# A state space mixer: the transposes of a group's inputs go behind its first projection, and VectorE scales the preceding group's output before it scales these inputs

## The chip, the cores and the metric

The kernel runs on one core of a Trainium2 chip. The time is the device time in microseconds of one execution; what is compared are medians of several executions. The engines named below are TensorE (PE in the rows; its weight loads are PEld), VectorE (DVE), ScalarE (ACT), GpSimd (POOL) and SyncE (SP, which only issues DMAs). All arithmetic is float32.

## The reference

One inference step of a two-layer decoder trunk, for a prompt of 512 tokens and for 8 samples with caches. Layer 0 is dilated attention beside gated linear attention, then an MLP. Layer 1 is the Mamba-2 state space mixer, then an MLP. The change lies in the mixer of layer 1:

```
z, xbc, dt = split_cols(h @ w_in, (C_INNER, C_CONV_DIM, C_HEADS))
conv = depthwise causal convolution of xbc over 4 taps
xbc_c = jax.nn.silu(conv + conv_b)
xs, bm, cm = split_cols(xbc_c, (C_INNER, C_GROUPS * C_STATE, C_GROUPS * C_STATE))
...
xdt = x * dt[..., None]
cb = einsum('bntgk,bnsgk->bngts', cm, bm)
y_intra = einsum('bngts,bngjts,bnsgjp->bntgjp', cb, seg, xdt)
u = einsum('bnsgk,bnsgj,bnsgjp->nbgjpk', bm, to_end, xdt)
...
y = y + d_skip[:, None] * xs
y = y.reshape(bsz, t_len, C_INNER) * jax.nn.silu(z)
y = rms_norm(y per group, w_gnorm)
```

There are 8 groups of 4 heads; a group has 256 channels of `x`, 128 of `B`, 128 of `C`, 256 of `z`. The 512 prompt tokens form four chunks of 128.

## The kernel before

Features lie on partitions and tokens along the free axis (520 columns: 512 of the prompt, 8 samples). A projection unit (`unit`, L535) multiplies 1024 features by 128 output columns in 16 matmuls, 8 for columns 0 to 259 and 8 for 260 to 519; its 512 KB of weights come by DMA into a ring of slots (`ring`). Each group needs six units: two for `x`, one for `B`, one for `C`, two for `z`.

The mixer is a software pipeline over groups. While group g is mixed, the six units of group g+1 are projected. Every engine has its own program, written out in order, with semaphores between them; groups 1 to 6 are a loop of three rounds with two groups each, groups 0 and 7 stand outside.

TensorE runs `ssd_mix`: transposes of `B` and of the samples (`ssd_tokens`, L966, L968) and of the inputs `x` (L974) from features to tokens, unit 0, the product of `C` and `B` (`ssd_cb`, L982), units 1 and 2, unit 3 with the samples' little products between its matmuls (`sample_y`, L995), the products inside and between chunks (L1011, L1016, L1025) among units 4 and 5, and last the sums of squares for the norm of the group's output (`ssd_norm`, L1032). In the last group `out_ahead` (L1089), the first part of the output projection, takes the place of the units.

The transposed `x` goes to PSUM banks 4 and 5. The same banks have just held the sums of squares of the preceding group, which ScalarE reads for its roots `ystd` (L1405, L1407); so the transposes wait for the semaphores `y_std_low` and `y_std`, which ScalarE gives.

VectorE runs `mix`: it copies the group's table (`tabg`, L1971) and the samples' rows (`ssamp`, L1975), scales these by dt (`sxdt`, L1976), scales the transposed `x` by dt (`xdt`, L1981, two instructions that read banks 4 and 5), then `normed` for the preceding group: a reciprocal (`yrstd`, L1948) and two products (`yout`, L1950, which read `yT` and `yrstd` from SBUF). Then the skip product (L1996), `prepare` and `taps` for the next group (L1898 to L1910: the convolution of one block of 128 channels, which needs that ScalarE has copied that unit's bank to `xe`), `xde` (L2000), `cbm` (L2003), `finish` (L1916, which needs ScalarE's tanh), the second block's taps, and `step_states` (L1992), eight instructions that step the samples' states `ss0`. TensorE's unit 3 waits for these (semaphore `ssm_stepped`, in `sample_y`).

GpSimd runs `states`: once `sxdt` is written it sends it to DRAM and back with a broadcast (L484, L488), and then multiplies the samples' states by their decays in two instructions on `ss0` (L496); it also sends states out and in.

The loops' order is only that of the code; nothing reorders it. The lines of the change:

```
dve.wait_ge(sem("x_turned"), g + 1)          # before xdt
dve.wait_ge(sem("y_std"), g + 1)             # at the start of normed
pe.wait_ge(sem("y_std" if t else "y_std_low"), g)   # before the transposes of x
pe.wait_ge(sem("ssm_stepped"), g * 2 + 2)    # in sample_y, before unit 3
```

Of the kernel before, what the change touches and what calls it, by code (L numbers as in the profile page):

```python
# [16 lines left out]
ALU = mybir.AluOpType  # L17
# [3 lines left out]
P = 128  # L21
# [23 lines left out]
CG, CHD, CN = 8, 64, 128  # L45
CJ = 4
# [97 lines left out]
def build(nc, A):  # L144
    ctx = ExitStack()
    with ctx:
        sems = {}

        def sem(name):
            if name not in sems:  # L150
                sems[name] = ctx.enter_context(nc.semaphore(name))
            return sems[name]

        def sb(name, shape, dt=F32, stack=ctx):
            return stack.enter_context(nc.sbuf_tensor(name, shape, dt))
# [123 lines left out]
        xdt = sb("xdt", [P, NT, CJ, CHD], stack=c)  # L279
# [243 lines left out]
        def _(pe):  # L523
            mm = nc.tensor.matmul

            def unit(w, n, s, count, src, first=0, last=True, start=True, ready=None, blocks=range(DC), used=True,
                     between=None):


                pe.wait_ge(ring_in[s], count * 16)  # L530
                for cols, half in MATMULS:
                    for k in blocks:
                        if ready is not None:
                            pe.wait_ge(*ready(k, cols.start > 0))
                        x = mm(half(n), ring[:, s, k], src[:, first + k, cols],  # L535
                               start=start and k == blocks[0], stop=last and k == blocks[-1])
                        if between is not None and not (cols.start and k == blocks[-1]):
                            between(k + DC * (cols.start > 0))
                x.then_inc(units_multiplied if used else sem("parts_multiplied"), 1)

            def bank_free(n, more=0):

                if n >= 2:
                    pe.wait_ge(copied[n % 2], turns_before(n) + more)
# [8 lines left out]
            def normed(r):  # L553

                return lambda k, high: (hn_ready, HN_BEFORE[r] + k + 1 + (0 if r in LATE_ROOT else DC * high))
# [7 lines left out]
            def project():  # L563

                w = at[0]
                if w >= U_OUT0:
                    return
                at[0] += 1
                n = T_ATT + w if w < U_GLA else T_GLA + w - U_GLA
                if w == U_GLA:  # L570
                    gates()
                bank_free(n)
                unit(w, n, w % RING, w // RING + 1, hn,
                     ready=normed(0) if w == 0 else None)

            def gates():

                n = T_GATE
                bank_free(n)
                pe.wait_ge(late_consts_in, 16 * len(LATE_CONSTS))  # L580
                for cols, half in MATMULS:
                    for k in range(DC):
                        x = mm(half(n)[0:RANK], wglow[:, k], hn[:, k, cols], start=k == 0, stop=k == DC - 1)
                x.then_inc(sem("glow_summed"), 1)
# [377 lines left out]
            def ssd_tokens(g, d):  # L962

                pe.wait_ge(sem("conv_ready"), g + 1)
                for t in range(NT):
                    pe.transpose(B[6][:, t * P:(t + 1) * P], conv[:, d, 2, t * P:(t + 1) * P], ident[:])  # L966
                for i in range(2):
                    x = pe.transpose(B[7][0:NB, i * P:(i + 1) * P], conv[:, d, i, TP:T], ident[:])  # L968
                x.then_inc(sem("ssd_turned"), 1)
                for t in range(NT):  # L970
                    if t % 2 == 0 and (not isinstance(g, int) or g > 0):
                        pe.wait_ge(sem("y_std" if t else "y_std_low"), g)
                    for i in range(2):
                        x = pe.transpose(B[4 + t // 2][:, (t % 2) * GW + i * P:(t % 2) * GW + (i + 1) * P],  # L974
                                         conv[:, d, i, t * P:(t + 1) * P], ident[:])
                x.then_inc(sem("x_turned"), 1)

            def ssd_cb(g, d):

                pe.wait_ge(sem("btok_ready"), g + 1)  # L980
                for t in range(NT):
                    x = mm(B[6][:, t * P:(t + 1) * P], conv[:, d, 2, t * P:(t + 1) * P],  # L982
                           conv[:, d, 3, t * P:(t + 1) * P], start=True, stop=True)
                x.then_inc(sem("cb_ready"), 1)

            def sample_y(g, d, products):


                pe.wait_ge(sem("cbm_ready"), g + 1)
                pe.wait_ge(sem("ssm_stepped"), g * 2 + 2)  # L990

                def some(m):
                    for n in range(m * 2 * NB // (products - 1), (m + 1) * 2 * NB // (products - 1)):
                        i, b = n // NB, n % NB
                        x = mm(B[6][:, n:n + 1], flat(ss0[:, b, 2 * i:2 * i + 2, :]),  # L995
                               conv[:, d, 3, TP + b:TP + b + 1], start=True, stop=True, skip_group_check=True)
                        if n == 2 * NB - 1:
                            x.then_inc(sem("ssm_read"), 1)
                return some
# [20 lines left out]
            def ssd_inter(g, d):  # L1020

                pe.wait_ge(sem("states_kept"), g + 1)
                for t in range(1, NT):
                    for i in range(2):
                        x = mm(B[4 + i][:, t * P:(t + 1) * P], flat(st[:, t - 1, 2 * i:2 * i + 2]),  # L1025
                               conv[:, d, 3, t * P:(t + 1) * P], start=True, stop=True)
                x.then_inc(sem("y_inter"), 1)
# [7 lines left out]
            def ssd_mix(g, d, project, products=2 * DC):  # L1035

                if not isinstance(g, int) or g > 0:
                    pe.wait_ge(sem("y_read"), g)
                ssd_tokens(g, d)
                project(0)  # L1040
                ssd_cb(g, d)
                project(1)
                project(2)
                project(3, sample_y(g, d, products))
                ssd_intra(g)
                project(4)
                ssd_inter(g, d)
                project(5)
                ssd_norm(g)
# [389 lines left out]
        def _(dve):  # L1439
            V = nc.vector  # L1440
# [451 lines left out]
            def mdo(ins, name=None):  # L1892
                mix_tally.done(ins, mstep if name is None else sem(name))

            def prepare(g, d):

                conv_tally.start("conv", g)
                cdo(V.tensor_scalar(pg[:, d, 0:20], parm[:, g, 0:20], 0.5, None, ALU.mult))  # L1898
                cdo(V.tensor_copy(pg[:, d, 20:24], parm[:, g, 20:24]))
                cdo(V.tensor_copy(xs[:, :, 0:3, :], parm[:, g, 24:120].rearrange("p (c t b) -> p c t b", c=4, t=3)))  # L1900

            def taps(g, d, j):

                n = T_SSD + j
                dve.wait_ge(copied[n % 2], g * (SSD_UNITS // 2) + (turns_before(n) + 1))
                out = conv[:, d, j, 0:TP]
                cdo(V.tensor_scalar(out, xe[:, j, 0:TP], pg[:, d, 4 * j:4 * j + 1], pg[:, d, 16 + j:17 + j],
                                    ALU.mult, ALU.add))
                for tap in range(1, TAPS):
                    cdo(V.scalar_tensor_tensor(out, xe[:, j, tap:tap + TP], pg[:, d, 4 * j + tap:4 * j + tap + 1],  # L1910
                                               out, ALU.mult, ALU.add), "taps_done" if tap == TAPS - 1 else None)
# [46 lines left out]
            def pair(i):  # L1958
                return B[i][:].rearrange("p (t j q) -> p t j q", t=2, j=CJ)
# [5 lines left out]
            def mix(g, d, nxt, prev):  # L1965
                mix_tally.start("mix", g)
                dve.wait_ge(sem("ssd_turned"), g + 1)
                if prev is not None:
# [3 lines left out]
                steps = tabg[:, F_DT:F_CUM].rearrange("p (t j) -> p t j", j=CJ)  # L1972
# [3 lines left out]
                mdo(V.tensor_tensor(sxdt[:], ssamp[:].rearrange("b i (j q) -> b (i j) q", j=2),  # L1976
                                    steps[0:NB, NT].unsqueeze(2).to_broadcast((NB, CJ, CHD)), ALU.mult),
                    "sxdt_ready")
                dve.wait_ge(sem("x_turned"), g + 1)
                for i in range(2):  # L1980
                    mdo(V.tensor_tensor(xdt[:, 2 * i:2 * i + 2], pair(4 + i),  # L1981
                                        steps[:, 2 * i:2 * i + 2].unsqueeze(3).to_broadcast((P, 2, CJ, CHD)),
                                        ALU.mult), "xdt_ready" if i else None)
                if prev is not None:
                    normed(prev, 1 - d)
                def step_states(half):
# [9 lines left out]
                    mdo(V.tensor_scalar(yT[:, i], conv[:, d, i], pg[:, d, 20 + i:21 + i], None, ALU.mult))  # L1996
                if nxt is not None:
                    prepare(nxt, 1 - d)
                    taps(nxt, 1 - d, 0)
                mdo(V.tensor_tensor(xde, xdt[:], toend[:].unsqueeze(3).to_broadcast((P, NT, CJ, CHD)),  # L2000
                                    ALU.mult), "xde_ready")
# [257 lines left out]
```

## Time and profile before

| | |
|---|---|
| median of 3 executions | 1883.25 us (1878.39, 1883.25, 1883.38) |
| the profiled execution | 1877.73 us, of which the span is 1875.9 us |
| busy over the span | TensorE 95%, its weight loads 81%, VectorE 54%, ScalarE 21%, GpSimd 7% |
| mean granted TensorE clock | 0.963 of full speed |
| the mixer's eight groups | about 923 to 1384 us of the span |

TensorE is busy nearly throughout, so the time is its work plus the stops in it. An engine with a lower share matters only where TensorE waits for it. In the timeline rows the first number is the start and the second the duration, from the first instruction of the merged row to the end of its last; in brackets stands how long the engine was idle before it and who released it. A matmul in float32 leaves two records, so a unit of 16 matmuls shows as x32.

### The profile page before, as it was taken

What the parts mean: (1) busy time and instruction counts of PE and PEld (TensorE: products, weight loads), DVE (VectorE), ACT (ScalarE), POOL (GpSimd) and SP (SyncE); (2) the same over time, 40 slices, a digit from 0 to 9 for tenths busy, and PEclk for the clock granted to TensorE, in tenths of its full rate; (3) what the DMA queues carried; (4) which work ended last, traced back from release to release, by engine and by line L of the source; (5) the groups of instructions that cost most, each with busy time, mean ns of one, the idle gap of its engine ahead of it and who ended that gap; (6) DMA issues with size and microseconds to landing.
All of it is one profiled execution on the core that took longest, in us unless ns stands there. A gap on an engine that the chain in (4) does not pass through costs nothing.

```text
span 1875.9 us, 23013 instructions
## 1 busy us (share of the span) xinstructions
PE 1783.4 (95%) x8520; PEld 1512.1 (81%) x8520; DVE 1018.9 (54%) x1889; ACT 389.1 (21%) x964; POOL 128.9 (7%) x205
## 2 busy tenths in 40 slices
PE   6999999997999999998999999999999999999995
PEld 5776688776888888887888888888878888888884
DVE  4443762437554445445477777777652543454554
ACT  2332101101220023100143432334310230012100
POOL 1000210000000000000101111101100000000001
PEclk9999968878999999998999999999999999999997
DMA  7111532103654675551333343432322332443211
GB/s 253 63 56 46 177 109 63 36 13 112 238 199 153 239 284 216 195 203 34 132 131 113 118 146 137 148 126 101 140 100 79 141 137 115 157 157 135 96 62 46
DMA packets 50168, 244.25 MB, mean 130 GB/s; under 512 B 7544, under 2 KB 10696, under 8 KB 44960
## 3 DMA queue, kind: packets, MB, share of 16 engines
q1 hardware_dynamic: 37312, 123.74, 19.4%
q0 software_dynamic: 12624, 119.21, 16.5%
q8 instruction: 60, 0.98, 0.2%
q14 instruction: 28, 0.23, 0.1%
q10 hardware_dynamic: 144, 0.09, 0.0%
HBM read 227.56 MB, written 82.53 MB: 165 GB/s over the span
## 4 chain that ended last, share of the span: by engine, by line
PE 84%; DVE 9%; DMA 2%; issue 2%; ACT 2%; POOL 0%; DVEq 0%; ACTq 0%; SPq 0%
PE bank L922 41%; PE bank L535 28%; PE bank L1089 2%; PE bank L677 1%; DVE ss L1992 1%; DVE conv L1910 1%; PE bank L1011 1%; PE bank L637 1%; PE bank L621 1%; PE bank L995 1%; DVE rstd L1450 1%; PE bank L1016 1%; DMA ring<-units 1%; DVE yrstd L1948 1%; DMA gath<-cache_v 1%
## 5 line engine op out<-in xcount | busy, mean ns | idle before, releaser
L535 PE MATMUL bank<-hn,ring 128*128 128x260 f32 x2304 | 552.8, 394 | 13.4 <-DVE ss L1992 6.5
L535 PEld LDWEIGHTS bank<-hn,ring 128*128 128x128 f32 x2304 | 434.6, 194 | 87.8 <-issue 16.1
L922 PE MATMUL bank<-hid,ring 128*128 128x260 f32 x1024 | 231.0, 383 | 0.0
L922 PEld LDWEIGHTS bank<-hid,ring 128*128 128x128 f32 x1024 | 194.7, 190 | 29.7
L922 PE MATMUL bank<-hid,ssum 128*128 128x260 f32 x768 | 174.2, 382 | 0.0
L922 PEld LDWEIGHTS bank<-hid,ssum 128*128 128x128 f32 x768 | 146.0, 190 | 22.3
L922 PE MATMUL bank<-hn,ring 128*128 128x260 f32 x512 | 125.1, 387 | 5.6 <-DVE hnt L1727 5.6
L922 PE MATMUL bank<-hnt,ring 128*128 128x260 f32 x512 | 123.5, 383 | 0.0
L1747 DVE TENSOR_TENSOR u<-bank,p1c 128x260 f32<-128x260 f32 x48 | 20.6, 429 | 185.1 <-PE bank L922 183.5
L922 PE MATMUL bank<-hnt,ssum 128*128 128x260 f32 x512 | 118.9, 385 | 1.8 <-DVE hid L1756 1.8
L922 PEld LDWEIGHTS bank<-hn,ring 128*128 128x128 f32 x512 | 98.4, 193 | 21.6 <-DVE hnt L1727 6.4
L922 PEld LDWEIGHTS bank<-hnt,ssum 128*128 128x128 f32 x512 | 97.8, 191 | 17.3 <-DVE hid L1756 2.2
L922 PEld LDWEIGHTS bank<-hnt,ring 128*128 128x128 f32 x512 | 97.6, 191 | 15.0
L1290 ACT ACTIVATE hid<-hid 128x260 f32<-128x260 f32 x96 | 40.3, 420 | 258.2 <-DVE hid L1753 178.4
L1752 DVE TENSOR_TENSOR u<-bank,u 128x260 f32<-128x260 f32 x48 | 20.6, 428 | 122.9 <-PE bank L922 122.6
L1137 ACT ACTIVATE hn<-h 128x520 f32<-128x520 f32 x40 | 25.0, 635 | 261.2 <-DVE h L1783 153.4
L1910 DVE SCALAR_TENSOR_TENSOR conv<-xe,pg,conv 128x512 f32<-128x512 f32 x96 | 72.2, 752 | 3.4
L535 PE MATMUL bank<-mixT,ring 128*128 128x260 f32 x224 | 60.7, 433 | 9.4 <-DVE h L1699 9.3
L1302 ACT ACTIVATE p1c<-bank 128x260 f32<-128x260 f32 x48 | 18.6, 387 | 244.9 <-PE bank L922 244.9
L535 PEld LDWEIGHTS bank<-mixT,ring 128*128 128x128 f32 x224 | 47.5, 216 | 23.6 <-DVE h L1699 11.8
L922 PE MATMUL bank<-hn,ssum 128*128 128x260 f32 x256 | 61.3, 382 | 0.0
L535 PE MATMUL bank<-yout,ring 128*128 128x260 f32 x256 | 56.4, 383 | 2.4 <-DVE h L1699 2.4
(341 smaller groups left out, 2188.7 us busy)
## 6 DMA issues: line engine op xcount, KB each, us to landing
ring<-units SPq DMA_DIRECT2D x224, 512.0 KB, 4.1
seg<-cums POOLq DMA_DIRECT2D x8, 1024.0 KB, 4.8
ss<-ssm POOLq DMA_DIRECT2D x8, 1024.0 KB, 7.5
xb<-sxs POOLq DMA_DIRECT2D x8, 1024.0 KB, 5.0
out_ssm<-ss POOLq DMA_DIRECT2D x8, 1024.0 KB, 5.8
out_win_k<-cache_k POOLq DMA_DIRECT2D x8, 1022.0 KB, 8.5
out_win_v<-cache_v POOLq DMA_DIRECT2D x8, 1022.0 KB, 6.3
gath<-cache_k POOLq DMA_DIRECT2D x24, 256.0 KB, 3.9
```

What stands on the lines that cost most here:

```text
L535: x = mm(half(n), ring[:, s, k], src[:, first + k, cols], start=start and k == blocks[0], stop=last and k == blocks[-1])
L621: mm(B[4 + j][:, 0:(j + 1) * P], qr[rows, j * P:(j + 1) * P], kr[rows, 0:(j + 1) * P], start=True, stop=True).then_inc(sem("scored"), 1)
L637: mm(B[7][AD * e:AD * e + AD, kt * P:TP], vtok[:, kt, AD * e:AD * e + AD], pt[:, PT_AT[kt]:PT_AT[kt] + TP - kt * P], start=kt == 0, stop=k ...
L677: x = mm(out[:, hp, b, :], gath[:, n % SLOTS, i, hp * P:(hp + 1) * P], spt[:, i, b * AH + 2 * hp:b * AH + 2 * hp + 2], start=b == 0 and hp ...
L922: x = mm(bank[:, 0:LO], weight(m, w, q % (DC // 2)), operand(m, q), start=q == 0 and m not in (2, 3), stop=q == every - 1, skip_group_chec ...
L995: x = mm(B[6][:, n:n + 1], flat(ss0[:, b, 2 * i:2 * i + 2, :]), conv[:, d, 3, TP + b:TP + b + 1], start=True, stop=True, skip_group_check= ...
L1089: x = mm(bank(n), ring[:, w, k], yout[:, part * DC + k, cols], start=part == 0 and k == 0, stop=part == 1 and k == DC - 3, skip_group_chec ...
L1137: run(hn[:, k], h[:, k], ACT.Square).then_inc(squares, 1)
L1290: ins = run(out, src, ACT.Relu)
L1747: do(V.tensor_tensor(u2[:], B[5][:, 0:LO], p1c[:], ALU.add), "banks_read")
L1752: do(V.tensor_tensor(u3[:], B[7][:, 0:LO], u2[:], ALU.add), "banks_read")
L1910: cdo(V.scalar_tensor_tensor(out, xe[:, j, tap:tap + TP], pg[:, d, 4 * j + tap:4 * j + tap + 1], out, ALU.mult, ALU.add), "taps_done" if t ...
```

## The change

On TensorE the eight transposes of `x` leave `ssd_tokens` and become `ssd_inputs`, called behind `project(0)`. Their waits for `y_std_low` and `y_std` go with them. On VectorE the wait for `x_turned` and the two `xdt` products go behind `normed`, the skip product and `prepare`, ahead of the first `taps`. The other engines' programs are the same. No instruction is added or removed.

```
--- before.py
+++ after.py
@@ ssd_tokens
                 x.then_inc(sem("ssd_turned"), 1)
+
+            def ssd_inputs(g, d):
+
                 for t in range(NT):
                     if t % 2 == 0 and (not isinstance(g, int) or g > 0):
                         pe.wait_ge(sem("y_std" if t else "y_std_low"), g)
@@ ssd_mix
                 ssd_tokens(g, d)
                 project(0)
+                ssd_inputs(g, d)
                 ssd_cb(g, d)
@@ mix on VectorE
-                dve.wait_ge(sem("x_turned"), g + 1)
-                for i in range(2):
-                    mdo(V.tensor_tensor(xdt[:, 2 * i:2 * i + 2], pair(4 + i),
-                                        steps[:, 2 * i:2 * i + 2].unsqueeze(3).to_broadcast((P, 2, CJ, CHD)),
-                                        ALU.mult), "xdt_ready" if i else None)
                 if prev is not None:
                     normed(prev, 1 - d)
@@ mix on VectorE, behind the skip product
                 if nxt is not None:
                     prepare(nxt, 1 - d)
+                dve.wait_ge(sem("x_turned"), g + 1)
+                for i in range(2):
+                    mdo(V.tensor_tensor(xdt[:, 2 * i:2 * i + 2], pair(4 + i),
+                                        steps[:, 2 * i:2 * i + 2].unsqueeze(3).to_broadcast((P, 2, CJ, CHD)),
+                                        ALU.mult), "xdt_ready" if i else None)
+                if nxt is not None:
                     taps(nxt, 1 - d, 0)
```

TensorE at the start of a group of the loop, before: L966 and L968 are the transposes of `B` and of the samples, L974 those of `x`, L535 unit 0, L982 the product of `C` and `B`.

```order
L966 MATMUL bank<-ident,conv 128x128 x3
L968 MATMUL bank<-ident,conv 8x128 x2
L974 MATMUL bank<-ident,conv 128x128 [waits y_std_low]
...
L974 MATMUL bank<-ident,conv 128x128 [waits y_std]
...
L535 MATMUL bank<-hn,ring 128x260 [waits ring0_in]
L535 MATMUL bank<-hn,ring 128x260 x15
L982 MATMUL bank<-conv 128x128 [waits btok_ready]
```

The same place after the change, where L977 is the old L974 and L985 the old L982.

```order
L966 MATMUL bank<-ident,conv 128x128 x3
L968 MATMUL bank<-ident,conv 8x128 x2
...
L535 MATMUL bank<-hn,ring 128x260 [waits ring0_in]
L535 MATMUL bank<-hn,ring 128x260 x15
L977 MATMUL bank<-ident,conv 128x128 [waits y_std_low]
...
L977 MATMUL bank<-ident,conv 128x128 [waits y_std]
...
L985 MATMUL bank<-conv 128x128 [waits btok_ready]
```

The transposes of `x` and both their waits have moved past the 16 matmuls of unit 0.

VectorE at the start of a group of the loop, before: from the samples' product to the first tap of the next group.

```order
L1976 TENSOR_TENSOR sxdt<-ssamp,tabg 8x256 [waits ssamp_read]
L1981 TENSOR_TENSOR xdt<-bank,tabg 128x512 [waits x_turned,sxdt_ready]
...
L1981 TENSOR_TENSOR xdt<-bank,tabg 128x512 [waits vec_ssd_step]
L1948 RECIPROCAL yrstd<-ystd 128x520 [waits y_std,xdt_ready]
...
L1950 SCALAR_TENSOR_TENSOR yout<-yT,pg,yrstd 128x520
...
L1996 TENSOR_SCALAR yT<-conv,pg 128x520 [waits yout_ready]
...
L1900 COPY xs<-parm 128x4x24
...
L1907 TENSOR_SCALAR conv<-xe,pg 128x512 [waits pair0_copied]
```

The same place after the change (L1980 is the old L1976, L1952 and L1954 are L1948 and L1950, L1995 is L1996, L1904 is L1900, L2000 is L1981, L1911 is L1907).

```order
L1980 TENSOR_TENSOR sxdt<-ssamp,tabg 8x256 [waits ssamp_read]
L1952 RECIPROCAL yrstd<-ystd 128x520 [waits y_std,sxdt_ready]
...
L1954 SCALAR_TENSOR_TENSOR yout<-yT,pg,yrstd 128x520
...
L1995 TENSOR_SCALAR yT<-conv,pg 128x520 [waits yout_ready]
...
L1904 COPY xs<-parm 128x4x24
...
L2000 TENSOR_TENSOR xdt<-bank,tabg 128x512 [waits x_turned,vec_conv_step]
...
L2000 TENSOR_TENSOR xdt<-bank,tabg 128x512 [waits vec_ssd_step]
...
L1911 TENSOR_SCALAR conv<-xe,pg 128x512 [waits pair0_copied]
```

The reciprocal follows the samples' product directly, and the two `xdt` products stand between `prepare` and the first tap.

## Rows read from the trace of the kernel before

**Rows 1.** The page's first line.
```profile
span 1875.9 us, 23013 instructions
```

**Rows 2.** Timeline: the sums of squares that close groups 0 and 6.
```profile
980.48 1.04 PE L1032 MATMUL bank<-turns,normc 128*128 128x260 f32 x4
1324.81 1.04 PE L1032 MATMUL bank<-turns,normc 128*128 128x260 f32 x4
```

**Rows 3.** All waits of TensorE's matmuls from 980 to 1330 us: total, times, longest.
```profile
PE bank L974 <- ACT ystd L1405: 7.7, 7, 1.1
PE bank L535 <- DVE ss L1992: 6.5, 6, 1.2
```

**Rows 4.** Timeline of TensorE in group 3.
```profile
1098.05 1.09 PE L974 MATMUL bank<-ident,conv 128*128 128x128 f32 x8 [1.11 <-ACT ystd L1405]
1098.98 7.18 PE L535 MATMUL bank<-hn,ring 128*128 128x260 f32 x32
...
1106.89 14.19 PE L535 MATMUL bank<-hn,ring 128*128 128x260 f32 x64
...
1122.25 0.70 PE L535 MATMUL bank<-hn,ring 128*128 128x260 f32 x2 [1.17 <-DVE ss L1992]
```

**Rows 5.** Timeline of VectorE in group 3, with ScalarE and GpSimd beside it.
```profile
1097.90 0.47 ACT L1407 ACTIVATE ystd<-bank,normc 128x260 f32<-128x260 f32 x1
1097.98 0.41 DVE L1976 TENSOR_TENSOR sxdt<-ssamp,tabg 8x256 f32<-8x256 f32 x1
...
1099.25 1.42 DVE L1981 TENSOR_TENSOR xdt<-bank,tabg 128x512 f32<-128x512 f32 x2 [0.86 <-PE bank L974]
...
1100.70 3.40 DVE L1948 RECIPROCAL yrstd<-ystd 128x520 f32<-128x520 f32 x1
1101.12 3.77 POOL L496 TENSOR_TENSOR ss<-ss,tab 128x1024 f32<-128x1024 f32 x2
1104.27 1.20 DVE L1950 SCALAR_TENSOR_TENSOR yout<-yT,pg,yrstd 128x520 f32 x1 [0.16 <-DVE yrstd L1948]
1105.62 0.76 DVE L1950 SCALAR_TENSOR_TENSOR yout<-yT,pg,yrstd 128x520 f32 x1 [0.16 <-DVE yout L1950]
...
1108.56 0.55 DVE L1907 TENSOR_SCALAR conv<-xe,pg 128x512 f32<-128x512 f32 x1
...
1113.59 0.69 DVE L1916 SCALAR_TENSOR_TENSOR conv<-th,conv 128x512 f32<-128x512 f32 x1
1114.10 0.39 ACT L1337 ACTIVATE xe<-bank 128x260 f32<-128x260 f32 x1 [0.62 <-PE bank L535]
...
1114.94 0.55 DVE L1907 TENSOR_SCALAR conv<-xe,pg 128x512 f32<-128x512 f32 x1 [0.65 <-ACT xs L1339]
```

**Rows 6.** Timeline of VectorE beside GpSimd in group 7, then in group 0.
```profile
1333.23 3.77 POOL L496 TENSOR_TENSOR ss<-ss,tab 128x1024 f32<-128x1024 f32 x2
1333.70 3.86 DVE L1950 SCALAR_TENSOR_TENSOR yout<-yT,pg,yrstd 128x520 f32<-128x520 f32 x1
...
933.18 3.77 POOL L496 TENSOR_TENSOR ss<-ss,tab 128x1024 f32<-128x1024 f32 x2
934.95 2.30 DVE L1907 TENSOR_SCALAR conv<-xe,pg 128x512 f32<-128x512 f32 x1 [5.71 <-ACT xs L1339]
```

**Rows 7.** Timeline: TensorE behind two longer stops, and unit 0 of group 0.
```profile
374.39 1.92 PE L535 MATMUL bank<-mixT,ring 128*128 128x260 f32 x5 [2.99 <-DVE h L1699]
...
1400.48 0.70 PE L535 MATMUL bank<-yout,ring 128*128 128x260 f32 x2 [2.36 <-DVE h L1699]
...
925.79 8.28 PE L535 MATMUL bank<-hn,ring 128*128 128x260 f32 x32
```

**Rows 8.** Stretches: length, busy by engine (instructions), granted clock, DMA share, GB/s.
```profile
375.10:378.40 3.30, 3.30 (x9) 2.54 (x9) 3.06 (x8) 0.00 (x0) 0.00 (x0) 0.50 0.00 0
1400.50:1404.00 3.50, 3.50 (x16) 3.06 (x17) 2.13 (x5) 1.24 (x2) 0.00 (x0) 1.00 0.97 394
859.80:866.50 6.70, 4.83 (x11) 3.88 (x12) 6.63 (x12) 1.06 (x1) 0.00 (x0) 0.50 0.00 0
```

## The prediction, made before the changed kernel ran

> **What bounds the kernel now.** I read the page first, then all waits of TensorE inside the mixer, then one group's timeline. TensorE bounds the kernel, so only its stops and its pace count. The mixer is regular: groups 1 to 6 take (1324.81 - 980.48) / 6 = 57.4 us each [rows 2]. In this stretch TensorE's matmuls stop at two places and no others [rows 3]. The first is ahead of the transposes of `x`, 1.1 us in each group, for ScalarE's root. The second is ahead of unit 3, about 1.1 us in each of six groups, for VectorE's `step_states`. The reader is to see in group 3 that both stops lie on one line: TensorE could run from the samples' transposes to the end of unit 2 without VectorE, and then waits at 1121.08 until 1122.25 [rows 4]. So what TensorE gains ahead of unit 3 is worth nothing in groups 1 to 6 unless VectorE reaches the end of `step_states` earlier too. VectorE's chain from `sxdt` to there decides.
>
> **TensorE's part of the change.** The eight transposes no longer wait for the root, since unit 0 (7.18 us) now covers it. The saving is the 1.11 us of idle time and some of the refilling behind it; I take 1.26 us, the time by which the transposes start later than their place in the stream. In groups 1 to 6 this lengthens the stop ahead of unit 3 by as much. In group 7 nothing waits for VectorE until the output is normalised, so there it counts: -1.3 us. In group 0 there is no root to wait for, only a permutation. Unit 0's weights were asked for long before, and its slot is given back 2.2 us earlier, which nobody needs. What is late next: `xdt`, since the transposes now end at about 1098.05 - 1.26 + 7.18 + 0.92 = 1104.9 in group 3 instead of 1099.1.
>
> **VectorE's part, in group 3.** Before, `xdt` waits 0.86 us for the transposes, takes 1.42 us, and the reciprocal starts at 1100.70 [rows 5]. Now the reciprocal can start when `sxdt` and the root are done (1098.39 and 1098.37), say at 1098.45, and ends at 1101.85. With the 0.16 us of hand-over the first `yout` product starts at 1102.0, some 2.25 us earlier than at 1104.27. That is the whole offer of the change to VectorE.
>
> The offer is not taken up, and this is the step on which my forecast rests. GpSimd scales the states from 1101.12 to 1104.89 (L496, its start set by `sxdt` and a small DMA, which the change leaves where they are). The first `yout` took 1.20 us there and the second, with GpSimd quiet, 0.76 us. The first ended 0.58 us after GpSimd's end. In group 7 it started 0.47 us into GpSimd's work and took 3.86 us, ending at 1337.56, 0.56 us after GpSimd's end at 1337.00 [rows 6]. In group 0 a tap that takes 0.55 us took 2.30 us and ended 0.30 us after GpSimd's 936.95. The reciprocal lies wholly under GpSimd in group 3 and takes 3.40 us, so it is not held. So a `yout` that finds GpSimd at work is held till both its instructions are done. Started at 1102.0 it ends again at about 1105.47, now lasting 3.4 us. The two sides: unheld, it would end at 1102.8 (the 0.76 us row); held, at 1105.5 (the 3.86 us row is its exact likeness). I take held.
>
> Then the second `yout`, the skip product and `prepare` run as before, and `xdt` takes the place at 1108.56 where the first tap stood. The transposes (1104.9) are no wait. The tap starts 1.45 us later (1.42 and a hand-over). `xde`, `cbm` and `finish` follow with it: 1113.59 + 0.69 + 1.45 = 1115.7. The second block's taps waited 0.65 us for ScalarE's copy of unit 1, and unit 1 is now earlier; but ScalarE must first end its tanh, which follows the first taps, and needs 0.84 us from the copy's start to the tap's [rows 5], about 1115.8. So the second taps start at 1115.8 instead of 1114.94: 0.85 us later. `step_states` follows it without a wait, and unit 3 starts 0.85 us later. Six groups: 6 x 0.85 = +5.1 us. Everything behind unit 3 hangs on TensorE, or on ScalarE and VectorE work that is shifted alike.
>
> In group 0 `xdt` has no `normed` ahead of it. It waits for the transposes until about 934.1 (925.79 + 8.28 [rows 7], the place where unit 0 now ends), and runs to 935.5 beside GpSimd; the first tap then starts 0.6 us later than at 934.95, but is held until 937.25 in any case. No trace here shows `xdt`, which reads one operand from PSUM, beside GpSimd. If it isn't held the cost is 0; if it is held like the tap, `xdt` ends near 938.7, the tap 2 us later than now, and about 1.5 us reach unit 3. I take 0, by the reciprocal's row, which has one SBUF input too.
>
> The Trainium skill (SBUF — State Buffer, "Who interferes with whom") says that VectorE and GpSimd share one pair of ports as an exclusive lock, that whoever issues first keeps it for its whole instruction, and that a VectorE instruction with at most one SBUF input outside the two-port modes does not contend. By that rule the cost in group 0 is 0, against up to 1.5 us by the tap's row; and the rule speaks against this change, for it makes an earlier `yout` the loser. On `yout` and the reciprocal this trace agrees (3.86 and 3.40 us).
>
> **TensorE's clock.** The stop ahead of unit 3 grows from 1.17 us by 1.26 and 0.85 to 3.3 us, in each of six groups. Stops of 1.0 to 1.2 us leave the granted clock at 1.0 (2.4 GHz) through the whole mixer. The five stops of 2.98 to 4.86 us elsewhere (one stands in [rows 7]) were each followed by a stretch at 0.50 (1.2 GHz), the shortest 3.3 to 3.4 us [rows 8]; one of 2.36 us was not. Behind 3.3 us I expect the fall. A stretch of 3.4 us at half speed loses 1.7 us if all of it falls on matmuls; unit 0 of group 0, which lies partly in one, took 8.28 us against 7.18, a loss of 1.1. I take 1.4 us: 6 x 1.4 = +8.4 us. The ends are 0, and 3.3 us each for the long stretch of 6.7 us. Nothing covers it, since unit 3 and what follows pace the group.
>
> **The sum.** 5.1 - 1.3 + 0 + 8.4 = +12.2 us. On the profiled execution that is a span of 1875.9 + 12.2 = 1888.1 us [rows 1] and 1877.7 + 12.2 = 1889.9 us in all. That execution lies 5.5 us below the median of the runs, so for the median: 1883.25 + 12.2 = 1895.4, say 1895 us.
>
> **Rivals.**
> - *Held, but the clock stays up.* `yout` gains nothing, `xdt` delays the taps, TensorE stops 3.3 us and goes on at 2.4 GHz. For it: one stop of 2.36 us went by without a fall, and unit 3 is steady work on both sides. Against it: all five longer stops. Time: 1883.25 + 3.8 = 1887 us.
> - *Not held: faster.* One mechanism: GpSimd's L496 starts behind the first `yout`, because the small DMA of `sxdt` lands later, or it is GpSimd that waits. It decides from a start of L496 at 1102.0 in group 3, 0.9 us later than now. For it: in group 7 L496 starts only 0.47 us before `yout`, in group 3 3.15 us before, so that DMA can be 2.7 us slower. Against it: in the loop its source and its neighbours don't move. Then `yout` ends at 1103.7, `prepare` at about 1105.8, `xdt` waits for nothing and the first tap starts at 1107.3, 1.2 us earlier; unit 1 is 1.26 us earlier too. Six groups: -7.2, group 7 -1.3: -8.5 us, 1875 us.
> - *Worse.* Long half-clock stretches and a held `xdt` in group 0: 5.1 + 1.5 - 1.3 + 6 x 3.3 = +25 us, 1908 us.
>
> **How the numbers follow.** A measurement of this kernel tells 0.3% (5.6 us) from no change. Held and clock down 0.61; held and clock up 0.20; not held 0.12; worse 0.07. Of the likeliest case its own range is 1888 to 1902 (clock down in half of the groups, up to a full 1.7 us in each and a little more for the base, whose runs differ by 5 us). To hold 8 in 10 the range goes from 1882 to 1903, which takes in the second case and leaves out the third and the last. Faster 0.12 is the third case. Same 0.26 is the second case and 0.06 of the first, where the clock falls in one or two groups only. Slower 0.62 is the rest.
>
> **What would show it.** In the changed kernel's profile the first `yout` of groups 1 to 6 lasts about 3.4 us and ends 0.6 us after L496; the transposes' wait for `ystd` is gone; `xdt` starts without a wait some 9.3 us later than it did; the wait of unit 3 for `ss` is about 3.2 us, six times; the granted clock is 0.50 for some 3.4 us in each group right behind it; the period is about 59.6 us. I am wrong if `yout` lasts 0.76 us there, or if the clock row of the mixer stays at 1.00.

## The result and the profile after

The changed kernel takes 1932.27 us (median of 6, 1920.27 to 1939.02) against 1880.68 us for the kernel before on the same chip. The ratio is 1.0266, with a 95% interval of 1.0245 to 1.0288: 2.7% slower, some 50 us. The forecast was 1895 us, 12 us slower. It had the direction and the chain of causes right, and a quarter of the size.

The page's first line, in answer to [rows 1]:

```profile
span 1932.6 us, 23013 instructions
```

Timeline, the sums of squares that close groups 0 to 7 without group 4 (L1035 is the old L1032), in answer to [rows 2]:

```profile
990.39 1.04 PE L1035 MATMUL bank<-turns,normc 128*128 128x260 f32 x4
1058.67 1.04 PE L1035 MATMUL bank<-turns,normc 128*128 128x260 f32 x4
...
1127.08 1.04 PE L1035 MATMUL bank<-turns,normc 128*128 128x260 f32 x4
1187.09 1.04 PE L1035 MATMUL bank<-turns,normc 128*128 128x260 f32 x4
...
1324.84 1.04 PE L1035 MATMUL bank<-turns,normc 128*128 128x260 f32 x4
1382.89 1.04 PE L1035 MATMUL bank<-turns,normc 128*128 128x260 f32 x4
1439.37 1.04 PE L1035 MATMUL bank<-turns,normc 128*128 128x260 f32 x4
```

From the end of group 0 to that of group 6 it is now 1382.89 - 990.39 = 392.5 us instead of 344.3, 48.2 us more. The groups are no longer alike: group 1 takes 68.3 us, group 3 60.0, group 6 58.1. Group 7 takes 56.5 us, 1.3 less than before. The span grew by 56.7 us. The 9.8 us that are left over lie ahead of the mixer, in code that the change doesn't touch: its first transposes start at 933.54 instead of 923.63, and group 0 closes at 990.39 instead of 980.48, so group 0 itself takes 56.85 us in both kernels.

All waits of TensorE's matmuls in groups 1 to 6, in answer to [rows 3]:

```profile
PE bank L535 <- DVE ss L1991: 19.8, 6, 3.5
```

The wait for the root is gone, and the one ahead of unit 3 has grown from 1.1 to 3.3 us: 13.3 us more, and 6.6 us less at the root (the seventh of its waits was in group 7). That nets to 6.7 us. Some 42 us of the 48 are no wait. The stretches of the groups show them (columns as in [rows 8]):

```profile
990.00:1058.00 68.00, 64.61 (x302) 55.73 (x301) 45.94 (x74) 20.74 (x53) 7.05 (x8) 0.85 0.31 111
...
1127.00:1187.00 60.00, 56.66 (x304) 49.40 (x303) 45.91 (x74) 20.74 (x53) 7.05 (x8) 0.97 0.35 125
...
1324.80:1382.90 58.10, 55.04 (x304) 48.15 (x304) 45.80 (x74) 20.73 (x53) 7.03 (x8) 1.00 0.36 129
```

The same 302 to 304 matmul records take 64.6 us at a mean clock of 0.85, and 55.0 us at 1.00. Half-speed stretches, one behind each stop in groups 1 to 5:

```profile
1020.00:1040.40 20.40, 20.40 (x76) 17.32 (x75) 8.03 (x13) 5.44 (x17) 0.60 (x1) 0.50 0.11 41
1088.30:1108.60 20.30, 20.30 (x73) 17.12 (x74) 7.71 (x12) 5.74 (x18) 0.60 (x1) 0.50 0.11 40
1156.60:1159.80 3.20, 3.20 (x11) 2.62 (x11) 1.21 (x2) 1.92 (x7) 0.00 (x0) 0.50 0.00 0
1214.60:1238.30 23.70, 23.64 (x84) 20.08 (x85) 8.77 (x15) 7.39 (x23) 0.60 (x1) 0.50 0.10 35
1286.30:1306.60 20.30, 20.30 (x75) 17.22 (x75) 8.12 (x13) 5.32 (x17) 0.60 (x1) 0.50 0.13 44
sum 87.90, PE 87.84 PEld 74.36 DVE 33.84 ACT 25.81 POOL 2.41; mean PE 17.57 PEld 14.87 DVE 6.77 ACT 5.16 POOL 0.48
```

TensorE works through 88 us at 1.2 GHz and loses half of them, 44 us. With the 6.7 us of waits that is a little over the 48.2 us measured. In group 3 the clock came back after some 3.3 us; in group 6 it did not fall.

VectorE and GpSimd in group 1 (L1952 is the reciprocal, L1954 the output products, L2000 `xdt`, L1911 the first tap), in answer to [rows 5]:

```profile
993.61 3.40 DVE L1952 RECIPROCAL yrstd<-ystd 128x520 f32<-128x520 f32 x1
...
996.32 3.77 POOL L496 TENSOR_TENSOR ss<-ss,tab 128x1024 f32<-128x1024 f32 x2
997.17 3.49 DVE L1954 SCALAR_TENSOR_TENSOR yout<-yT,pg,yrstd 128x520 f32 x1 [0.16 <-DVE yrstd L1952]
1000.82 0.76 DVE L1954 SCALAR_TENSOR_TENSOR yout<-yT,pg,yrstd 128x520 f32 x1 [0.16 <-DVE yout L1954]
...
1003.65 1.42 DVE L2000 TENSOR_TENSOR xdt<-bank,tabg 128x512 f32<-128x512 f32 x2
1005.21 0.55 DVE L1911 TENSOR_SCALAR conv<-xe,pg 128x512 f32<-128x512 f32 x1
```

The first output product starts early and lasts 3.49 us, until 0.57 us after GpSimd's end at 1000.09. In five of the six groups it lasts 3.3 to 3.5 us. In group 2 the small DMA came late and GpSimd began behind the first output product; then the hold fell on the skip product (L1995) instead:

```profile
1065.45 0.76 DVE L1954 SCALAR_TENSOR_TENSOR yout<-yT,pg,yrstd 128x520 f32 x1 [0.16 <-DVE yrstd L1952]
...
1066.88 4.07 POOL L496 TENSOR_TENSOR ss<-ss,tab 128x1024 f32<-128x1024 f32 x2
...
1067.17 4.06 DVE L1995 TENSOR_SCALAR yT<-conv,pg 128x520 f32<-128x520 f32 x2
```

The two skip products took 4.06 us instead of 1.02. The stop of group 2 was the longest of all, 3.53 us.

### The profile page after: what moved, and what is told of

It is laid out like the page before. It is cut to its first block, busy times and chain, and to the rows that moved or that the text cites. A ratio compares the mean times of both kernels' runs of the same rounds, so it can differ in the third digit from the quotient of the medians.

```text
span 1932.6 us, 23013 instructions
## 1 busy us (share of the span) xinstructions
PE 1834.8 (95%) x8520; PEld 1551.4 (80%) x8520; DVE 1032.9 (53%) x1889; ACT 388.7 (20%) x964; POOL 129.4 (7%) x205
## 4 chain that ended last, share of the span: by engine, by line
PE 82%; DVE 11%; issue 2%; DMA 2%; ACT 2%; DVEq 0%; POOL 0%; ACTq 0%; SPq 0%
PE bank L922 40%; PE bank L535 27%; PE bank L1093 2%; DVE conv L1914 1%; PE bank L677 1%; PE bank L1014 1%; DVE yout L1954 1%; DVE yrstd L1952 1%; DVE ss L1991 1%; PE bank L998 1%; PE bank L637 1%; PE bank L621 1%; DVE rstd L1454 1%; PE bank L1019 1%; DMA ring<-units 1%
## 5 line engine op out<-in xcount | busy, mean ns | idle before, releaser
L535 PE MATMUL bank<-hn,ring 128*128 128x260 f32 x2304 | 589.9, 411 | 26.3 <-DVE ss L1991 19.8
L535 PEld LDWEIGHTS bank<-hn,ring 128*128 128x128 f32 x2304 | 451.3, 202 | 103.5 <-DVE ss L1991 22.2
L922 PE MATMUL bank<-hn,ring 128*128 128x260 f32 x512 | 125.1, 387 | 5.6 <-DVE hnt L1731 5.6
L922 PEld LDWEIGHTS bank<-hn,ring 128*128 128x128 f32 x512 | 98.3, 192 | 21.7 <-DVE hnt L1731 6.4
L998 PEld LDWEIGHTS bank<-conv,ss 128*128 128x128 f32 x256 | 64.2, 260 | 14.4
L535 PE MATMUL bank<-mixT,ring 128*128 128x260 f32 x224 | 60.7, 433 | 9.3 <-DVE h L1703 9.3
L535 PEld LDWEIGHTS bank<-mixT,ring 128*128 128x128 f32 x224 | 47.5, 216 | 23.6 <-DVE h L1703 11.8
```

The costliest lines, as they stand in the source:

```text
L535: x = mm(half(n), ring[:, s, k], src[:, first + k, cols], start=start and k == blocks[0], stop=last and k == blocks[-1])
L922: x = mm(bank[:, 0:LO], weight(m, w, q % (DC // 2)), operand(m, q), start=q == 0 and m not in (2, 3), stop=q == every - 1, skip_group_chec ...
```

## The experiments

The theory after the result, A: GpSimd's scaling holds VectorE's early output product, `xdt` comes on top, and TensorE's stop ahead of unit 3 passes 3 us; behind it the granted clock falls, and the mixture of unit 3 (a full matmul and a one-column product by turns) keeps it down until unit 3 is over. Rivals: the order costs by itself (B); the clock falls for another reason than the stop (C); the scaling has no part in it (D); or, on the length of the stretch, that the mixture has no part in it (A2).

**Spare matmuls in the stop.** The changed kernel, with

```
@@ sample_y, ahead of its waits
+                if not isinstance(g, int):
+                    pe.wait_ge(sem("xdt_ready"), g + 1)
+                    for _ in range(6):
+                        mm(B[5][:, 0:LO], ones, hn[:, 0, 0:LO], start=True, stop=True)
```

> The changed kernel, with six spare 128x260 matmuls into a PSUM bank that is free there, ahead of the wait of unit 3, in groups 1 to 6. They take 6 x 0.45 = 2.7 us of the 3.3 us in which TensorE stands there, so they cost no time by themselves; everything else is as in the changed kernel. Theory A (the stop lets the granted clock fall, and the half-speed stretch is what costs): the rest of the stop is 0.3 to 0.8 us, the clock of the mixer stays at 1.00, and the time is about the kernel before + 4 us (VectorE's 0.85 us in six groups, less 1.3 us in the last group), 1882 to 1887 us. Rival B (the loss lies in the order itself, in VectorE's held instructions and what follows them): nothing changes, 1920 to 1939 us. Rival C (TensorE's clock falls for another reason than the stop, such as the transposes' new place): half-clock stretches stay.

Measured: 1887.04 us (6 runs, 1885.57 to 1889.97), ratio to the kernel before 1.0028 (1.0015 to 1.0040). More work on the busiest engine made the changed kernel 45 us faster. The stretch of groups 1 to 6 and most of group 7 in its profile:

```profile
985.00:1386.00 401.00, 396.83 (x2171) 347.55 (x2170) 308.23 (x494) 139.15 (x352) 49.23 (x56) 1.00 0.35 126
```

The clock is 1.00 throughout. The same held products, the same `xdt`, the same place of the transposes now cost 5 us. Rivals B and C fall. (The whole stop was not filled: 4.2 us of waits are left over the six groups.)

**The little products in one piece.** The changed kernel, with

```
@@ ssd_mix
-                project(3, sample_y(g, d, products))
+                some = sample_y(g, d, 2)
+                project(3)
+                some(0)
```

> The changed kernel, with the samples' 16 little products behind unit 3 in one piece instead of one between each two of its matmuls; the wait of unit 3 for the stepped states stays where it is, so the stop of 3.3 us stays. Theory A1 (the stop starts the half-speed stretch, and the mixture of unit 3 is what keeps it for 20 us): unit 3 is now dense, the stretches last 3.4 us, the loss per group is about 1.7 us instead of 10, time 1890 to 1900 us. Rival A2 (the length has nothing to do with the mixture; once down the clock stays for some 20 us): as the changed kernel, 1920 to 1940 us. A third possibility: the 16 products in one piece, 3.4 us with hardly a column each, let the clock fall themselves, behind unit 3: then as long or longer stretches that begin there.

Measured: 1906.85 us (4 runs, 1897.9 to 1912.03), ratio 1.0119 (1.0091 to 1.0148). About half of the loss is gone, while TensorE's stops are as long as before (20.0 us over six). Group 2 of its profile, in three stretches:

```profile
1081.50:1088.20 6.70, 5.98 (x14) 4.73 (x15) 3.39 (x7) 4.49 (x15) 0.00 (x0) 0.50 0.00 0
1088.40:1095.00 6.60, 6.60 (x45) 6.08 (x43) 3.31 (x5) 3.56 (x10) 0.00 (x0) 1.00 0.22 64
1095.20:1101.90 6.70, 6.70 (x41) 6.26 (x42) 4.69 (x10) 0.86 (x2) 0.60 (x1) 0.51 0.41 166
```

Here the clock is down around the stop for 6.8 us and comes back while the dense unit 3 still runs; it is so in group 1 too, in groups 3, 4 and 6 it is down for 3.4 us, and in group 5 not at all. Then the 16 little products stand in one piece, and in groups 1, 2, 3 and 5 the clock falls in the last 1.3 us of that piece or within 1.4 us behind it, for another 3.4 to 6.8 us. So both A1 and the third possibility of the expectation took place.

**Few little products.** The changed kernel, without 13 of the 16 little products in each group (the samples' outputs are incomplete):

```
@@ sample_y, in the loop over the products
+                        if n < 2 * NB - 1 and n % NB:
+                            continue
```

> The changed kernel with 13 of the 16 little products of the samples left out in each group (three stay, one of them the last): so unit 3 is nearly all full matmuls, and nothing stands in one piece behind it either. The stop ahead of unit 3 stays at 3.3 us. Leaving them out saves TensorE 13 x 0.21 = 2.7 us in each of 8 groups, 22 us. Theory A1 (the mixture keeps the clock down): the half-speed stretches behind the stop last 3.4 us, at most 6.8; 6 x 1.7 = 10 us for them, so about 1880.7 + 3.8 + 10 - 22 = 1873 us. Rival A2 (once down, the clock stays for some 20 us whatever runs): stretches of 20 us, 10 us each: 1910 us or more.

Measured: 1885.51 us (one run; the kernel before beside it 1880.04). The stops are 19.6 us over six groups, as in the changed kernel. Groups 1 and 3 of its profile:

```profile
1017.70:1021.00 3.30, 3.30 (x10) 2.53 (x9) 0.93 (x2) 2.30 (x9) 0.00 (x0) 0.50 0.00 0
1021.20:1040.00 18.80, 18.80 (x114) 16.48 (x114) 15.42 (x31) 5.09 (x14) 2.21 (x4) 1.00 0.38 133
1130.30:1137.00 6.70, 5.71 (x14) 4.63 (x15) 3.61 (x6) 4.58 (x16) 0.00 (x0) 0.51 0.09 38
1137.20:1160.00 22.80, 22.80 (x133) 19.93 (x132) 17.89 (x35) 6.17 (x16) 2.21 (x4) 1.00 0.51 190
```

No half-speed stretch is longer than 6.8 us, one is 3.4 us, and two groups have none. A2 falls: with full matmuls behind the stop, the clock comes back. The time is 12 us over what was expected. Part of the 22 us did not come: TensorE, faster through unit 3, now waits 3.3 us over three groups for VectorE's sum of the samples' outputs. The rest was not traced.

**The kernel before with a delay.** Nothing of the change, but

```
@@ mix on VectorE, ahead of step_states(0)
+                if not isinstance(g, int):
+                    V.reciprocal(yrstd[:, 0:320], yrstd[:, 0:320]).then_inc(sem("delayed"), 1)
+                    dve.wait_ge(sem("delayed"), g)
```

> The kernel before, with one spare VectorE instruction of about 2.15 us (a reciprocal of 320 columns in place, on a buffer that is free there) ahead of the stepping of the states in groups 1 to 6. Nothing of the change is in it, but unit 3 now waits 1.1 + 2.15 = 3.3 us, as in the changed kernel. The delay itself costs 6 x 2.15 = 13 us. Theory A: the clock falls behind that stop and stays down through unit 3 in most groups, 10 us in each: 1880.7 + 13 + 20 to 60 = 1915 to 1955 us. Rivals B and C (the order of the change is needed for the loss): 1894 us, clock at 1.00.

Measured: 1952.9 us (4 runs, 1946.45 to 1961.95), ratio 1.0368 (1.0346 to 1.0391). The waits ahead of unit 3 are 19.6 us over six groups. The half-speed stretches of its six groups (the first, the second and the sum):

```profile
1017.00:1040.70 23.70, 23.70 (x92) 20.25 (x91) 9.18 (x15) 4.44 (x14) 0.60 (x1) 0.50 0.14 44
1088.70:1105.50 16.80, 16.80 (x53) 14.31 (x52) 5.57 (x8) 3.23 (x10) 0.00 (x0) 0.50 0.00 1
...
sum 128.80, PE 128.80 PEld 109.61 DVE 48.32 ACT 24.36 POOL 3.00; mean PE 21.47 PEld 18.27 DVE 8.05 ACT 4.06 POOL 0.50
```

Half of 128.8 is 64 us; with the 13 us of delay that is 77, and this execution lies 80 us above the median of the kernel before, 1882.36. The fall came in all six groups here. A stop of 3.3 us alone brings the loss, in the old order.

**VectorE's part alone.** TensorE transposes the inputs ahead of unit 0 as before; `xdt` stands behind `prepare`.

> VectorE's part of the change alone: the two products with dt stand behind the preceding group's output, the skip product and the preparation, while TensorE transposes the inputs ahead of unit 0 as before. Theory A with held products: the first output product lasts 3.4 us in groups 1 to 6, unit 3 starts 0.85 us later than in the kernel before, its stop grows from 1.1 to about 1.95 us (there is no gain of 1.26 us in front), which leaves the clock at 1.00: 5 us slower than before, 1884 to 1887 us. Rival B (the order on VectorE itself costs the 50 us): 1920 us or more. If the stop of 2 us already lets the clock fall: 1890 to 1930 us, with half-speed stretches behind it.

Measured: 1917.0 us (7 runs, 1889.36 to 1927.21). The executions lie 7 to 45 us above the median of the kernel before, 1882.36, so the median tells the size poorly. The mean granted clock goes with them: 0.959 in the fastest, 0.940 in the slowest. The profiled execution took 1919.86 us. The stops ahead of unit 3 are 11.7 us over six groups. In the profile, three groups have half-speed stretches of 20.4 us behind stops of 2.0 to 2.1 us; behind another stop of 2.0 us and two of 1.7 us there is none:

```profile
1017.50:1037.80 20.30, 20.30 (x77) 17.30 (x77) 8.32 (x13) 5.30 (x17) 0.60 (x1) 0.50 0.13 45
1085.70:1106.00 20.30, 20.30 (x77) 17.24 (x77) 8.16 (x13) 5.61 (x18) 0.60 (x1) 0.50 0.13 45
1154.00:1174.30 20.30, 20.30 (x77) 17.30 (x77) 8.36 (x13) 5.30 (x17) 0.60 (x1) 0.50 0.13 45
1218.00:1440.00 222.00, 211.51 (x1156) 184.04 (x1154) 157.41 (x255) 71.86 (x180) 23.33 (x28) 1.00 0.32 117
```

I had expected a stop of 2 us to leave the clock up. It did so in one group of four.

**The same with spare matmuls.** VectorE's part alone, and three spare matmuls as in the first experiment.

> VectorE's part of the change alone, as before, with three spare 128x260 matmuls (1.35 us) in groups 1 to 6 inside the 2 us for which TensorE stands ahead of unit 3. Theory A (the spread of that kernel's times, 1889 to 1927 us, is the clock that falls in some groups and not in others; the order itself costs 6 x 0.85 us): the clock of the mixer stays at 1.00, the times agree with each other within 0.5%, and the median is 5 us above the kernel before, 1885 to 1888 us. Rival: times that spread up to 1927 us as without the spare matmuls.

Measured: 1888.58 us (7 runs, 1886.27 to 1893.4), ratio 1.0039 (1.0018 to 1.0060). The clock of the mixer is 1.00, and the times lie within 0.4%. The held order costs 6 to 7 us by itself, and the spread of the kernel without the spare matmuls was the clock.

**A short scaling.** The changed kernel; GpSimd scales one sample instead of four in each of its two instructions (six samples stay without decay).

```
@@ states on GpSimd
-                for half in (slice(0, NB // 2), slice(NB // 2, NB)):
+                for half in (slice(0, 1), slice(NB // 2, NB // 2 + 1)):
```

> The changed kernel with GpSimd's scaling of the samples' states cut: each of its two instructions scales one sample instead of four, so the decay of six of the eight samples is left out; all else is as in the changed kernel. Theory A (the preceding group's output products are held by GpSimd's scaling, and that makes the stop long enough for the clock to fall): the first output product takes 0.76 us instead of 3.4 us in groups 1 to 6, the first tap comes some 1.2 us earlier than in the kernel before, unit 3 stops 1.2 us instead of 3.3, the clock stays at 1.00 in the mixer: 1871 to 1876 us, faster than the kernel before. Rival D (GpSimd has no part in it; the longer product has another cause, or the order costs by itself): the product stays at 3.4 us, the stop at 3.3 us, 1920 us or more.

Measured: 1873.42 us (5 runs, 1869.23 to 1877.78), ratio 0.9953 (0.9929 to 0.9977). The groups of the output products and of the scaling in its profile (mean ns of one in the second figure):

```profile
L1954 DVE SCALAR_TENSOR_TENSOR yout<-yT,pg,yrstd 128x520 f32 (+1 forms) x14 | 12.0, 856 | 2.0 <-DVE yrstd L1952 1.0 <-DVE yout L1954 1.0
L496 POOL TENSOR_TENSOR ss<-ss,tab 128x256 f32<-128x256 f32 x14 | 9.3, 692 | 0.1
```

The output products of groups 1 to 7 take 0.86 us on the mean (1.99 us in the changed kernel), the stop ahead of unit 3 is 1.1 us again, and the changed kernel is 0.5% faster than the one before. D falls: the same order gains 9 us or loses 50, by GpSimd's scaling alone.

**The scaling in another place.** The changed kernel with the whole computation; in groups 1 to 7 the first half of the scaling comes when the preceding group's squares are added, the second behind the first small DMA, under VectorE's reciprocal (`decay(half)` is the old instruction).

```
@@ states on GpSimd
+                if g:
+                    pool.wait_ge(sem("ssm_in"), g * 16 + 16)
+                    pool.wait_ge(sem("ysq_ready"), g)
+                    decay(low)
                 pool.wait_ge(sem("sxdt_ready"), g + 1)
                 pool.dma_start(sxs[g] ...)
+                if g:
+                    decay(high)
                 pool.wait_ge(sem("rows_out"), g * 16 + 32)
```

> The changed kernel with the whole scaling kept but placed elsewhere in GpSimd's program: in groups 1 to 7 its first half comes when the preceding group's squares are added (ysq_ready), its second half right behind the DMA that sends the samples' product away, ahead of the wait for that DMA, so that it lies under VectorE's reciprocal, which is not held. Theory A: the output products take 0.76 us each, the first tap is 1.2 us earlier than in the kernel before, the stop ahead of unit 3 is 1.1 to 1.3 us, clock at 1.00: 1871 to 1876 us, some 0.4% faster than the kernel before. Rival D: as the changed kernel, 1920 us or more. If the early half holds VectorE's gating or table copy instead, part of it is lost: 1877 to 1885 us.

Measured: 1874.22 us (10 runs, 1866.93 to 1878.34), ratio 0.9948 (0.9929 to 0.9966). This version is faster than both kernels, by 0.5% against the one before. Group 3 of its profile (L1963 is the reciprocal, L1965 the output products, L487 the scaling, L2011 `xdt`, L1922 the first tap):

```profile
1097.16 3.40 DVE L1963 RECIPROCAL yrstd<-ystd 128x520 f32<-128x520 f32 x1
...
1097.94 1.91 POOL L487 TENSOR_TENSOR ss<-ss,tab 128x1024 f32<-128x1024 f32 x1
...
1100.72 0.76 DVE L1965 SCALAR_TENSOR_TENSOR yout<-yT,pg,yrstd 128x520 f32 x1 [0.16 <-DVE yrstd L1963]
1101.64 0.76 DVE L1965 SCALAR_TENSOR_TENSOR yout<-yT,pg,yrstd 128x520 f32 x1 [0.16 <-DVE yout L1965]
...
1104.46 1.42 DVE L2011 TENSOR_TENSOR xdt<-bank,tabg 128x512 f32<-128x512 f32 x2
1106.02 0.55 DVE L1922 TENSOR_SCALAR conv<-xe,pg 128x512 f32<-128x512 f32 x1
```

GpSimd's second half ends at 1099.85, ahead of the first output product. The reciprocal above it keeps its 3.40 us. The first tap stands 8.9 us behind the reciprocal's start, against 11.6 us in the changed kernel.

**That place in the old order.** The kernel before with the same new place of the scaling.

> The kernel before with the same new place of the scaling, and none of the change. The first output product should take 0.76 instead of 1.2 us, but the second block's taps wait 0.3 to 0.75 us for unit 1 in any case, and TensorE's wait for the root stays: no difference, 1878 to 1883 us. If it is faster by 0.4% like the other kernel of this pair, the gain comes from GpSimd's place alone and the change adds nothing to it.

Measured: 1883.69 us (12 runs), ratio 1.0015 (0.9991 to 1.0040): no difference. So neither the change nor the scaling's new place gains alone. TensorE's two waits are what they were, 7.7 us at the root and 6.5 us ahead of unit 3; in the kernel with both, the first is gone, the second is still 6.5 us, and groups 1 to 3 of its profile take 56.0 to 56.2 us instead of 57.3 to 57.5. The new place with only one half of the change was not tried.

**TensorE's part alone.** `ssd_inputs` behind unit 0; VectorE's order as before.

> TensorE's part of the change alone: the inputs are transposed behind unit 0, while VectorE still scales them with dt ahead of the preceding group's output. VectorE then waits for the transposes until the end of unit 0, 5.7 us later than before; less the hold of the output product (0.45 us) and the wait for unit 1 (0.65 us) unit 3 starts some 4.6 us later in six groups, and its stop grows to 1.1 + 1.26 + 4.6 = 7 us, with the clock down behind it for the length of unit 3. 6 x 4.6 - 1.3 + 6 x 10 to 12 = +86 to +98: 1967 to 1979 us. If the clock does not matter: 1907 us.

Measured: 1984.93 us in one run. The waits ahead of unit 3 are 42.2 us over six groups, 7.0 us each, and the half-speed stretches 27 to 31 us. It is 6 us beyond the upper end of what was expected. In one execution it lies 53 us above the changed kernel, so the TensorE half of the change should not stand without the VectorE half.

## Why the prediction was wrong

- **TensorE's part**: right. The root's wait is gone, group 7 gained 1.3 us, and groups 1 to 6 gained nothing from it.
- **Held output product**: right in five of six groups (3.3 to 3.5 us). The Trainium skill's rule on what contends (SBUF — State Buffer, "Who interferes with whom") agrees with most of it: the output product with two SBUF inputs was held, the reciprocal and, in group 0, `xdt` with its PSUM operand were not. The skip product and the tap, which have one, were held; the rule leaves that open for the two-port modes, and no run here shows the mode. The row for `xdt` beside GpSimd, which no trace showed before:

```profile
943.21 3.78 POOL L496 TENSOR_TENSOR ss<-ss,tab 128x1024 f32<-128x1024 f32 x2
...
944.09 1.42 DVE L2000 TENSOR_TENSOR xdt<-bank,tabg 128x512 f32<-128x512 f32 x2 [6.73 <-PE bank L977]
```

  The skill's other part, that whoever issues first keeps the ports, does not fit group 7 by these records. There the second output product started 0.39 us ahead of GpSimd's scaling and was held all the same, until 0.56 us after GpSimd's end at 1394.51; it cost nothing, since nothing waits there.

```profile
1390.35 4.73 DVE L1954 SCALAR_TENSOR_TENSOR yout<-yT,pg,yrstd 128x520 f32<-128x520 f32 x1
...
1390.74 3.77 POOL L496 TENSOR_TENSOR ss<-ss,tab 128x1024 f32<-128x1024 f32 x2
```

- **The shift of 0.85 us a group, +3.8 us with group 7**: about right. With the clock kept up by spare matmuls it was 5 us, and group 6, the only one without a fall, took 58.05 us, 0.75 us more than its 57.30 before. Group 0 cost nothing, as forecast.
- **The stop of 3.3 us and the fall of the clock**: right, in five of six groups.
- **The size of that fall: here it failed.** The step was "I take 1.4 us: 6 x 1.4 = +8.4 us. The ends are 0, and 3.3 us each". It measured 44 us in all, 7.3 us a group on the mean of six, over twice the upper end. I took the length of a half-speed stretch from other places of the trace, where full matmuls follow the stop: 3.4 us as the rule, 6.7 as the worst. Behind this stop comes unit 3, in which every full matmul is followed by a product of one column. There the clock stayed down for 20 to 24 us in four of the five groups, until unit 3 had ended. The few-products kernel (3.4 to 6.8 us, one execution) and the one-piece kernel (the same, and a second fall at the end of the piece) show that the mixture does it. Longer ones stood in the same trace, and I passed over them: 13.5 us and 47.7 us in the attention stage, the second nearly all 128x2 matmuls. A stop of 2.37 us, at 442.89, behind which the clock was down, stood there too; the prediction names only the one of 2.36 us that went by without a fall.

```profile
248.80:296.50 47.70, 45.56 (x207) 44.68 (x207) 24.47 (x32) 1.23 (x2) 10.23 (x19) 0.50 0.36 110
...
443.40:446.70 3.30, 2.95 (x7) 1.71 (x6) 3.09 (x6) 0.11 (x1) 0.00 (x0) 0.50 0.15 60
```

- **The rival "not held: faster"** was priced wrongly in one point: in group 2 GpSimd did begin behind the output product, and nothing was won, since the skip product was held in its stead; in group 7 the second output product was. It is GpSimd's whole scaling that must go, as the short and the early scaling showed. Then its 1875 us was right (1873.4 and 1874.2).

What stays open: why the clock fell in some groups and not in others behind equal stops (2.0 us in the VectorE-only kernel; 3.06 us in groups 4 and 6 of the changed one), and why group 3 came back after some 3.3 us within the same mixture. The length of the stop does not settle it: a stop of 2.36 us at one place of the output projection, with the same work around it, was followed by some 3.3 us at 0.50 in the profiles of the short and the early scaling, and by none in those of the kernel before and of the changed one.

## What to carry to other kernels

A stop on TensorE can have two prices: its own length, and a half-speed stretch behind it, here 3.4 to 6.8 us where full matmuls followed and mostly 17 to 24 us where full and one-column products took turns. Take the second from a place where the same kind of work follows, not from the mean of the trace. Before such a mixture even 2 us of waiting is worth avoiding (three of four such stops brought 20 us at half speed), and spare matmuls in a stop tell in one run how much of a loss is clock. When a VectorE instruction is moved up, look at what GpSimd does at its new time: here the reciprocal and `xdt` could lie beside GpSimd's scaling, and the output product and the skip product could not.

## What the runs showed of the hardware that I had not expected

- Behind a stop of 3.0 to 3.5 us, alternating 128x260 matmuls and one-column products ran at 1.2 GHz for 20 to 24 us in four of six groups of the changed kernel, and for 17 to 24 us in all six of the delayed one; the same mixture behind stops of 1.0 to 1.2 us ran at 2.4 GHz in every group of the kernel before.
- Sixteen one-column products in one piece, 3.4 us of them at full clock, bring a fall of the clock at their end or just behind it in four of six groups, though the profile shows no idle time of TensorE there.
- GpSimd's two scaling instructions hold the output product as one: started 0.85 us into the first, it is let go only 0.57 us after the second. The skip products of group 2 were let go between them: each took 2.01 us, and the first ended 0.29 us after GpSimd's first instruction.
